# Exp and Gelu ahead of the scaled copy of the head before, and a tenth ring place in place of kept query weights

## The chip, the cores and the metric

The kernel runs on one core of one Trainium2 chip. The metric is the device time of one execution in microseconds; the time before is the median of three runs. Engines are called by the names of the profile: PE (TensorE), DVE (VectorE), ACT (ScalarE), POOL (GpSimd), SP (SyncE). A suffix q is the engine's instruction queue, which also issues DMAs.

## What is computed

One layer of a decoder trunk, on 1024 prompt tokens and 8 x 8 sample tokens, width 1024, all in 32-bit floats. The reference, cut down:

```python
z = x @ w_in                      # q, k, v (8 heads x 64), GLU value and gate (512 each)
att  = dilated window attention   # branches (128,1), (512,4), (2048,16), merged by their denominators
conv = silu(layer_norm(depthwise_conv31(a * sigmoid(g)) + conv_b))
x1 = layer_norm(ALPHA * x + concat(att, conv) @ w_out)

# PEER(x1): product-key choice of experts, 8 heads x 16 experts for each token
q = (x1 @ w_query).reshape(T, 8, 2, 128)
s = einsum('thpc,hpkc->thpk', q, sub_keys)        # 128 keys a side
top_s, top_i = top_k(s, 16)                       # a side
best_s, best_j = top_k(all 16 x 16 sums, 16)      # 16 of 16384 experts
gate = softmax(best_s)
act  = gelu(x1 . expert_u[e])                     # one dot for each token and expert
out  = sum(gate * act * expert_v[e])
y = layer_norm(ALPHA * x1 + out)
```

Further outputs are the new key, value and convolution caches; most of those bytes are copied from DRAM to DRAM.

## The kernel before

**Tiles and places.** The tokens are cut into 9 tiles: 8 prompt tiles of 128 tokens (t = 0 to 7) and one sample tile of 64. All five instruction streams walk the same plan: for n from -1 to 9, for g in 32 groups, for i in 4 places. In round n the experts of tile n are worked off, one slot (one of the 128 experts of each token) at a place, while the front of tile m = n + 1 runs beside them: attention in groups 1 to 9 (one head a group), convolution, output projection and LayerNorm in groups 10 to 15, query projection and the choice of experts from group 15 on. Each stream issues its work of a place in a written order and waits on semaphores, so an instruction that waits holds everything behind it on its engine.

**Experts.** `gather(t, s)` on POOL (L618) fetches 128 rows of 8 KB (u and v of one expert for each token, 1 MB) into a ring of RING = 9 places. On DVE `dot(t, s)` (L1053) makes the dot with x1; after every second slot `gelu` on ACT (L770) applies Gelu to the two results. One place later `weigh` on DVE (L1061, L1064) multiplies by the gates and writes diagonal matrices, and `values_pair` on PE (L1396, L1399, L1403) adds the weighted v rows into PSUM and counts `pv`. A gather waits for the `pv` of the slot that held its ring place. So gelu stands at places i = 1 and 3, weigh and values_pair at i = 2 and 0. Tile 0 has a ring of 4 and `first_values` (L1071 to L1079) on DVE in place of weigh and values_pair.

**Attention of head h in group g.** PE `scores` (L1270, banks 2 and 3, end of group h) -> DVE `weights_max` (L952, L955, i = 2 of group h + 1) -> ACT `weights_exp` (L685, i = 2) -> PE `weights_T` (L1281, i = 3) -> ACT `weights_T` (L694, copy to pT) -> PE `values` (L1292, i = 1 of group h + 2, into bank 2) -> ACT `normalise` (L702, copy scaled by the reciprocal of the sum, i = 1). `values` writes bank 2, which holds the next head's scores until their maximum is taken, and so waits for `sm_done` of head h + 1. `scores` of head h + 2 waits for the scaled copy of head h. In ACT's stream of a group the order is: Gelu (i = 1), scaled copy of head g - 2, Exp of head g - 1 (i = 2), Gelu (i = 3), copy of the transposes of head g - 1 (i = 3). In PE's: values_pair (i = 0), values of head g - 2 (i = 1), values_pair (i = 2), weights_T of head g - 1 and scores of head g (i = 3). ACT also has `ln2_std` (L779), whose result DVE's `ln2_end` (L1106) waits for in group 2.

**Query weights.** Eight blocks of 1 MB, one a head. Block 0 is loaded once from SP's queue (L485) and kept in wq0 for all tiles. The others go through two buffers wq[h % 2], issued from ACT's queue: heads 1 and 2 by `route_loads` (L721) in group 12 (group 18 for the sample tile), head h + 2 after the copy of query h (L751, L753). `queries(m, h)` (L1360) reads them in groups 15, 17, 18, 20, 22, 24, 25 and 27 of a prompt tile.

Of the kernel before, what the change touches and what calls it, by code (L numbers as in the profile page):

```python
# [14 lines left out]
P = 128  # L15
D = 1024
KD = D // P
SEQ = 1024
NB, NT = 8, 8
NS = NB * NT  # L20
# [4 lines left out]
AW = H * E  # L25
# [11 lines left out]
PH = 8  # L37
# [3 lines left out]
KEYC = 128  # L41
# [8 lines left out]
KBLK = NKEY // P  # L50
KEYS = NKEY + NT

RING, FIRST_RING = 9, 4
Z_RING = 4
PAIRS = SLOTS // 2
ROW = 2 * D
# [123 lines left out]
def rows(n):  # L180
    return P if n < PT else NS
# [27 lines left out]
def build(nc, I, O):  # L209
# [5 lines left out]
    with ctx:  # L215
# [3 lines left out]
        def at(off, shape, dt=F32):  # L219
            names[0] += 1  # L220
            return nc.alloc_sbuf_tensor_at(f"t{names[0]}", shape, dt, offset=base + off)

        def sem(name):
            return ctx.enter_context(nc.semaphore(name))
# [22 lines left out]
        wq = at(o_s, [P, 2, KD, 2 * KEYC])  # L247
# [32 lines left out]
        o_l = o_x + 2 * D * 4  # L280
        swapped = at(o_s + 10240, [P, D])

        wq0 = at(o_l, [P, KD, 2 * KEYC])
        lnw2 = at(o_l + 2 * D * 4, [P, 2, D])
        o_k = o_l + 4 * D * 4
        skT = at(o_k, [P, PH * 2, NK])
        o_m = o_k + PH * 2 * NK * 4
        taken = [o_m]
# [37 lines left out]
        sig = at(o_st, [P, 2, 512])  # L326
        q_st = [at(o_st + (2 + i) * 512 * 4, [P, 512]) for i in range(2)]
        assert o_st + 4 * 512 * 4 <= o_x
        glu_st = at(o_l + 2 * D * 4, [P, 3, 512])
        vs = at(o_l + 2 * D * 4 + 3 * 512 * 4, [NS, AW])  # L330

        const_in = sem("const_in")
        bias_in = sem("bias_in")
# [4 lines left out]
        wout_in = sem("wout_in")  # L338
        sk_in = sem("sk_in")
        ln_in = sem("ln_in")  # L340
        wq0_in = sem("wq0_in")
        ln2_in = sem("ln2_in")
        proj_done = sem("proj_done")
        proj_evac = sem("proj_evac")
# [15 lines left out]
        wq_in = [sem(f"wq_in{i}") for i in range(2)]  # L360
# [106 lines left out]
        def _(sp):  # L467
# [14 lines left out]
            sp.dma_start(w_out[:, :, :], I["w_out_t"]).then_inc(wout_in, 16)  # L482
            sp.dma_start(skT[:, :, :], I["skT"]).then_inc(sk_in, 16)
            sp.dma_start(ln1T[:, :, :], I["ln1_t"]).then_inc(ln_in, 16)
            sp.dma_start(wq0[:, :, :], I["wq_t"][0]).then_inc(wq0_in, 16)  # L485

            def copy_cache(i):
                new, old = ((kc_o, I["cache_k_win"]), (vc_o, I["cache_v_win"]))[i % 2]
# [74 lines left out]
            for n in range(TILES + 1):  # L563
                m = n + 1
# [61 lines left out]
        def _(act):  # L626
            def evacuate(u):
                p, _, kind, i, tile = UNITS[u]
                t0, tn, sn = PASSES[p]
                w = tn + sn  # L630
# [50 lines left out]
            def weights_exp(m, h):  # L681
                u = PH * m + h
                L = (m + 1) * P
                act.wait_ge(nm_done, u + 1)
                act.activation(sm[:, u % 2, 0:L], sm[:, u % 2, 0:L], ACT.Exp, bias=soft[:, 2 + u % 2:3 + u % 2], scale=SCALE,  # L685
                               accum_out=soft[:, 4 + u % 2:5 + u % 2]).then_inc(exp_done, 1)

            def weights_T(m, h):
                u = PH * m + h
                L = (m + 1) * P  # L690
                act.wait_ge(p_tr, u + 1)
                if u:
                    act.wait_ge(pv_done, u)
                act.activation(pT[:, 0:L], psum[:, 4 * 512:4 * 512 + L], ACT.Copy).then_inc(pT_ready, 1)  # L694

            def normalise(m, h):
                u = PH * m + h
                act.wait_ge(rd_done, u + 1)
                act.wait_ge(pv_done, u + 1)
                if h == 0 and m:  # L700
                    act.wait_ge(att_tr, m)
                act.activation(att[:, h * E:(h + 1) * E], bank[2][:, 0:E], ACT.Copy, scale=soft[:, 12 + u % 2:13 + u % 2]).then_inc(att_done, 1)  # L702

            def attended(m):
                act.wait_ge(att_tr, m + 1)
                act.activation(mixedT[:, 0:CT, :], bank[4].rearrange("p (c q) -> p c q", c=CT), ACT.Copy).then_inc(att_T, 1)  # L706

            def conv_std(m):
                act.wait_ge(c_var, m + 1)
                act.activation(cstat[0:rows(m), 9:10], cstat[0:rows(m), 8:9], ACT.Sqrt).then_inc(c_std, 1)  # L710


            def route_loads(m):
                if m < PT:
                    act.wait_ge(s_done, PH * (m + 1))
                    act.wait_ge(p_tr, PH * (m + 1))
                else:
                    act.wait_ge(satt_T, 2 * NB)
                act.wait_ge(c_tr2, m + 1)
                for h in (1, 2):  # L720
                    act.dma_start(wq[:, h % 2, :, :], I["wq_t"][h]).then_inc(wq_in[h % 2], 16)  # L721

            def conv_swish(m):
                act.wait_ge(c_tr2, m + 1)
                for c in range(CT):
                    act.activation(mixedT[:, CT + c, 0:rows(m)], bank[2][:, c * P:c * P + rows(m)], ACT.Silu,
                                   bias=cwT[:, c, CK + 2:CK + 3], scale=cwT[:, c, CK + 1:CK + 2]).then_inc(c_T, 1)

            def ln1_std(m):
                act.wait_ge(l_var, m + 1)  # L730
                act.activation(stat[0:rows(m), 17:18], stat[0:rows(m), 16:17], ACT.Sqrt).then_inc(l_std, 1)
# [11 lines left out]
            def x1_rows(m):  # L743
                for half in range(2):
                    act.wait_ge(x1_back, 2 * m + half + 1)
                    act.activation(x1[m % 2][0:rows(m), half * 512:(half + 1) * 512], bank[4 + half][0:rows(m), :], ACT.Copy).then_inc(x1_done, 1)

            def query_copy(m, h):
                r = rows(m)
                act.wait_ge(a_q, PH * m + h + 1)  # L750
                act.activation(qh[:, h % 2, 0:2 * r], bank[2 + h % 2][:, 0:2 * r], ACT.Copy).then_inc(a_qc, 1)  # L751
                if 1 <= h < PH - 2:
                    act.dma_start(wq[:, h % 2, :, :], I["wq_t"][h + 2]).then_inc(wq_in[h % 2], 16)  # L753

            def score_copy(m, h):
# [72 lines left out]
                                x1_rows(PT)  # L828

            def front(m, g, i):  # L830
                if i == 1 and 2 <= g < PH + 2:
                    normalise(m, g - 2)
                if i == 2 and 1 <= g <= PH:
                    weights_exp(m, g - 1)
                if i == 3 and 1 <= g <= PH:
                    weights_T(m, g - 1)
                for h in range(PH):
                    if g == QUERY_AT[h] and i == 3:
                        query_copy(m, h)
                        if h == 0:  # L840
                            x1_rows(m)
                if i != 2:
                    return
                if g == 11:
                    conv_std(m)
                if g == 12:
                    conv_swish(m)
                    attended(m)
                    route_loads(m)
                if g == 14:  # L850
                    ln1_std(m)
                if g == 15:
                    x1_transposed(m)
                for h in range(PH):
                    if g == QUERY_AT[h] + 1:
                        score_copy(m, h)

            for n in range(-1, TILES + 1):
                m = n + 1
# [373 lines left out]
        def _(pe):  # L1233
# [114 lines left out]
            def queries(m, h):  # L1348
                r = rows(m)
                if h == 0:  # L1350
                    pe.wait_ge(x1T_ready, KD * (m + 1))

                if h == 0 and m == 0:
                    pe.wait_ge(wq0_in, 16)
                if h:
                    pe.wait_ge(wq_in[h % 2], 16 * ((4 * m + h // 2 + 1) if h % 2 else (3 * m + h // 2)))
                w_ = wq[:, h % 2, :, :] if h else wq0
                for side in range(2):
                    for k in range(KD):
                        last = pe.matmul(bank[2 + h % 2][:, side * r:(side + 1) * r], w_[:, k, side * KEYC:(side + 1) * KEYC],  # L1360
                                         x1T[:, k, 0:r], start=(k == 0), stop=(k == KD - 1))
                last.then_inc(a_q, 1)
# [119 lines left out]
                                x1_rows(PT)  # L1482

            def front(m, g, i):
                if i == 1 and 2 <= g < PH + 2:
                    values(m, g - 2)
                if i == 3 and 1 <= g < PH + 1:
                    weights_T(m, g - 1)
                if i == 3 and g < PH:
                    scores(m, g)  # L1490
                for h in range(PH):
                    if g == QUERY_AT[h] and i == 3:
                        queries(m, h)
                        if h == 0:
                            x1_rows(m)
                    if g == QUERY_AT[h] + 1 and i == 1:
                        key_scores(m, h)
                if g == 13 and i in (1, 3):
                    out_projection(m, i // 2)
                if i != 1:  # L1500
                    return
                if g == 10:
                    att_transposes(m)
                    conv_rows(m)
                if g == 12:
                    conv_back(m)
                if g == 15:
                    x1_transposes(m)

            for n in range(-1, TILES + 1):  # L1510
                m = n + 1
# [65 lines left out]
```

## Time and profile before

| | |
|---|---|
| median of 3 runs | 3743.29 us (3739.91 to 3750.01) |
| profiled execution | 3747.08 us, its span 3745.3 us |
| busy | DVE 75%, PE 69%, POOL 33%, ACT 18% |
| bytes moved | 1385.68 MB, of them 1140.92 MB by the gathers |
| round n = 0 (tile 0's experts) | from the first gather at 191 us to about 875 us |
| rounds n = 1 to 6 | about 875 to 3080 us |
| round n = 7 (tile 7's experts, sample attention) | about 3080 to 3480 us |
| sample tile's experts | to the end |

In the page and in the tables by stretches, PEclk is the granted TensorE clock as a share of full speed, DMA the mean busy share of the 16 DMA engines, GB/s what they moved. A wait's row reads: who waited, for whom, us in total, times, the longest. In a row of the timeline the number in brackets is the idle time of the engine just before, with what ended it.

### The profile page before, as it was taken

How to read it: one execution, taken by the hardware profiler on the slowest of the kernel's cores; microseconds unless marked ns; L12 is line 12 of the kernel's file. 1: busy time of each engine (PE TensorE's matmuls, PEld its weight loads, DVE VectorE, ACT ScalarE, POOL GpSimd, SP SyncE). 2: the span in 40 equal slices, each digit the busy share in tenths (PEclk: the TensorE clock that was granted, in tenths of full speed). 3: DMA queues.
4: the chain of work that ended last, by engine and by line, in shares of the span. 5: the costliest groups of instructions: out<-in, count | busy, mean ns of one | idle time of the engine just before them, and what ended most of it. 6: DMA issues, size and time to landing. Idle time of an engine off the chain costs nothing.

```text
span 3745.3 us, 39494 instructions
## 1 busy us (share of the span) xinstructions
PE 2592.0 (69%) x13744; PEld 1193.5 (32%) x13744; DVE 2799.2 (75%) x7472; ACT 681.2 (18%) x1478; POOL 1236.1 (33%) x1092
## 2 busy tenths in 40 slices
PE   7864347736775777677677766776787666779766
PEld 5433124532232223233323332333233322234311
DVE  5177867898789868986897689768976894356965
ACT  1210122002200321032013200320132002121000
POOL 0022212123443444434443434344434432233242
PEclk8987668867887888888788888887888878889889
DMA  9977898979999999999999999999989999999698
GB/s 341 343 296 258 303 371 311 400 278 355 398 417 381 361 381 421 395 367 375 415 391 347 381 421 390 344 369 421 393 336 368 420 409 422 418 420 396 261 384 342
DMA packets 217512, 1385.68 MB, mean 370 GB/s; under 512 B 27417, under 2 KB 38169, under 8 KB 66649
## 3 DMA queue, kind: packets, MB, share of 16 engines
q0 software_dynamic: 156672, 1140.92, 76.1%
q1 hardware_dynamic: 40384, 142.88, 10.4%
q10 hardware_dynamic: 20256, 99.35, 6.7%
q8 instruction: 109, 1.79, 0.2%
q14 instruction: 91, 0.74, 0.1%
HBM read 1369.94 MB, written 80.04 MB: 387 GB/s over the span
## 4 chain that ended last, share of the span: by engine, by line
DVE 30%; PE 26%; DMA 25%; issue 13%; ACT 3%; POOL 2%; ACTq 0%; SPq 0%; DVEq 0%; POOLq 0%
DMA t<-in_expert_uv,t 25%; PE psum L1403 12%; DVE t L1053 8%; PE psum L1250 3%; PE psum L1292 3%; DVE psum L1079 2%; PE psum L1328 2%; POOL t L618 2%; PE psum L1360 2%; DVE t L1064 2%; DVE t L1001 2%; DVE t L999 2%; PE psum L1270 2%; DVE t L1002 2%; DVE t L1000 1%
## 5 line engine op out<-in xcount | busy, mean ns | idle before, releaser
L618 POOL DMA_INDIRECT t<-in_expert_uv,t x1088 | 1235.9, 1136 | 2479.9 <-PE psum L1399 982.0
L1403 PE MATMUL psum<-t,t 64*64 64x512 f32 x4576 | 1323.4, 717 | 652.0 <-DVE t L1064 651.4
L1053 DVE CUSTOM_DVE_ANT_0 t<-t,t 128x1024 f32<-128x1024 f32 x1088 | 1322.2, 1222 | 529.6 <-DMA t<-in_expert_uv,t 520.0
L1399 PE MATMUL psum<-t,t 64*64 64x512 f32 x2592 | 807.9, 753 | 0.0
L1403 PEld LDWEIGHTS psum<-t,t 64*64 64x64 f32 x4576 | 329.0, 154 | 1422.6 <-DVE t L1064 798.4
L770 ACT ACTIVATE t<-t 128x2 f32<-128x2 f32 x544 | 110.6, 203 | 2038.0 <-DVE t L1053 2037.0
L1360 PEld LDWEIGHTS psum<-t,t 128*128 128x128 f32 x2304 | 286.3, 206 | 72.2 <-issue 63.4
L1360 PE MATMUL psum<-t,t 128*128 128x128 f32 (+1 forms) x2304 | 296.6, 291 | 4.8 <-ACT t L740 4.8
L1250 PE MATMUL psum<-t,t 128*128 128x128 f32 (+2 forms) x768 | 269.7, 512 | 6.6 <-DMA t<-in_xT 6.1
L920 DVE SCALAR_TENSOR_TENSOR t<-t,t,t 128x128 f32<-128x128 f32 x840 | 238.0, 346 | 0.0
L1292 PE MATMUL psum<-t,t 128*128 128x64 f32 x576 | 105.9, 348 | 162.7 <-issue 162.2
L1399 PEld LDWEIGHTS psum<-t,t 64*64 64x64 f32 x2592 | 182.3, 157 | 0.0
L1250 PEld LDWEIGHTS psum<-t,t 128*128 128x128 f32 x768 | 137.7, 210 | 123.3 <-issue 116.6
L1061 DVE TENSOR_TENSOR t<-t,t 128x2 f32<-128x2 f32 x480 | 75.9, 158 | 128.4 <-ACT t L770 126.3
L1079 DVE SCALAR_TENSOR_TENSOR psum<-t,t,psum 128x1024 f32<-128x1024 f32 x127 | 163.8, 1290 | 4.9 <-DVE t L1071 0.5
L1292 PEld LDWEIGHTS psum<-t,t 128*128 128x128 f32 x576 | 97.3, 256 | 211.1 <-issue 209.9
L1064 DVE TENSOR_TENSOR t<-t,t 128x128 f32<-128x128 f32 x480 | 140.2, 292 | 16.6
L1396 PE MATMUL psum<-t,t 128*64 128x512 f32 x256 | 118.9, 611 | 44.7 <-DVE t L1064 44.7
L1328 PE MATMUL psum<-t,t 128*128 128x512 f32 (+1 forms) x288 | 131.9, 614 | 3.6 <-ACT t L706 3.6
L770 ACT ACT_TABLE_LOAD x103 | 132.1, 1283 | 1.8
L1374 PE MATMUL psum<-t,t 128*128 128x128 f32 (+1 forms) x288 | 53.9, 316 | 112.4 <-ACT t L751 111.9
L1270 PE MATMUL psum<-t,t 64*128 64x512 f32 (+3 forms) x192 | 88.3, 571 | 39.7 <-DMA t<-q_scratch 39.2
(136 smaller groups left out, 2122.2 us busy)
## 6 DMA issues: line engine op xcount, KB each, us to landing
t<-in_wq_t ACTq DMA_DIRECT2D x63, 1024.0 KB, 9.6
out<-in_cache_k_win SPq DMA_DIRECT2D x8, 4080.0 KB, 46.2
out<-in_cache_v_win SPq DMA_DIRECT2D x8, 4080.0 KB, 40.9
t<-in_w_in_t ACTq DMA_DIRECT2D x44, 512.0 KB, 7.5
t<-in_kc_t SPq DMA_DIRECT2D x8, 2560.0 KB, 18.6
t<-in_vc_t SPq DMA_DIRECT2D x8, 2560.0 KB, 14.0
t<-in_expert_uv,t POOLq DMA_INDIRECT x1088, 11.0
t<-in_w_v_t ACTq DMA_DIRECT2D x6, 1024.0 KB, 10.0
```

The lines of the kernel that those rows point to most:

```text
L618: pool.indirect_dma_start(ring[:, r, :], None, I["expert_uv"], bass.IndirectOffsetOnAxis(ap=idn[t % 2][:, s:s + 1], axis=0)).then_inc(land ...
L770: act.activation(d_, d_, ACT.Gelu).then_inc(a_gelu, 1)
L920: dve.scalar_tensor_tensor(dst, src, w, dst, ALU.mult, ALU.add).then_inc(cv, 1)
L1053: dve.tensor_tensor_reduce(out=ring[:, r, 0:D], in0=x1[t % 2][:, :], in1=ring[:, r, 0:D], scale=1.0, scalar=0.0, op0=ALU.mult, op1=ALU.add ...
L1064: dve.tensor_tensor(zt[:, k % Z_RING, :, :], ident2[:, :].unsqueeze(1).broadcast_to([P, 2, NS]), d2.unsqueeze(2).broadcast_to([P, 2, NS]), ...
L1079: dve.scalar_tensor_tensor(first_sum, ring[:, r, D:ROW], w_, first_sum, ALU.mult, ALU.add).then_inc(v_done, 1)
L1250: last = pe.matmul(dst[:, 0:tn + sn], w_ring[:, r, k, :], xT[p][:, k, 0:tn + sn], start=(k == 0), stop=(k == KD - 1))
L1292: last = pe.matmul(bank[2][:, 0:E], pT[:, j * P:(j + 1) * P], v[:, j, h * E:(h + 1) * E], start=(j == 0), stop=(j == m))
L1328: last = pe.matmul(bank[3 - half][0:rows(m), :], mixedT[:, k, 0:rows(m)], w_out[:, k, half * 512:(half + 1) * 512], start=(k == 0), stop=( ...
L1360: last = pe.matmul(bank[2 + h % 2][:, side * r:(side + 1) * r], w_[:, k, side * KEYC:(side + 1) * KEYC], x1T[:, k, 0:r], start=(k == 0), s ...
L1399: last = pe.matmul(AUX[t][half][NS - NS * a:P - NS * a, :], zt[NS * a:NS * a + NS, k % Z_RING, j, :], vv[NS * a:NS * a + NS, :], start=(c ...
L1403: last = pe.matmul(MAIN[t][half][NS * a:NS * a + NS, :], zt[NS * a:NS * a + NS, k % Z_RING, j, :], vv[NS * a:NS * a + NS, :], start=(c == ...
```

## The change

Four edits. On ACT the scaled copy of head g - 2 moves from i = 1 to i = 3 of its group, behind the Exp of head g - 1 and the second Gelu and ahead of the copy of the transposes. On PE values of head g - 2 move from i = 1 to i = 3, behind the second values_pair and ahead of the transposes of head g - 1. Block 0 of the query weights is no longer kept: route_loads loads heads 0 and 1, and head 2 is loaded after the copy of query 0, like the ones after it. The 8 KB a partition that this frees becomes a tenth place of the ring; x1 and what lies behind it move up by as much, lnw2, glu_st and vs keep their addresses.

```diff
--- before.py
+++ after.py
@@ -50,7 +50,7 @@
 KBLK = NKEY // P
 KEYS = NKEY + NT
 
-RING, FIRST_RING = 9, 4
+RING, FIRST_RING = 10, 4
 Z_RING = 4
 PAIRS = SLOTS // 2
 ROW = 2 * D
@@ -280,9 +280,8 @@
         o_l = o_x + 2 * D * 4
         swapped = at(o_s + 10240, [P, D])
 
-        wq0 = at(o_l, [P, KD, 2 * KEYC])
-        lnw2 = at(o_l + 2 * D * 4, [P, 2, D])
-        o_k = o_l + 4 * D * 4
+        lnw2 = at(o_l, [P, 2, D])
+        o_k = o_l + 2 * D * 4
         skT = at(o_k, [P, PH * 2, NK])
         o_m = o_k + PH * 2 * NK * 4
         taken = [o_m]
@@ -326,8 +325,8 @@
         sig = at(o_st, [P, 2, 512])
         q_st = [at(o_st + (2 + i) * 512 * 4, [P, 512]) for i in range(2)]
         assert o_st + 4 * 512 * 4 <= o_x
-        glu_st = at(o_l + 2 * D * 4, [P, 3, 512])
-        vs = at(o_l + 2 * D * 4 + 3 * 512 * 4, [NS, AW])
+        glu_st = at(o_l, [P, 3, 512])
+        vs = at(o_l + 3 * 512 * 4, [NS, AW])
 
         const_in = sem("const_in")
         bias_in = sem("bias_in")
@@ -338,7 +337,6 @@
         wout_in = sem("wout_in")
         sk_in = sem("sk_in")
         ln_in = sem("ln_in")
-        wq0_in = sem("wq0_in")
         ln2_in = sem("ln2_in")
         proj_done = sem("proj_done")
         proj_evac = sem("proj_evac")
@@ -482,7 +480,6 @@
             sp.dma_start(w_out[:, :, :], I["w_out_t"]).then_inc(wout_in, 16)
             sp.dma_start(skT[:, :, :], I["skT"]).then_inc(sk_in, 16)
             sp.dma_start(ln1T[:, :, :], I["ln1_t"]).then_inc(ln_in, 16)
-            sp.dma_start(wq0[:, :, :], I["wq_t"][0]).then_inc(wq0_in, 16)
 
             def copy_cache(i):
                 new, old = ((kc_o, I["cache_k_win"]), (vc_o, I["cache_v_win"]))[i % 2]
@@ -717,7 +714,7 @@
                 else:
                     act.wait_ge(satt_T, 2 * NB)
                 act.wait_ge(c_tr2, m + 1)
-                for h in (1, 2):
+                for h in (0, 1):
                     act.dma_start(wq[:, h % 2, :, :], I["wq_t"][h]).then_inc(wq_in[h % 2], 16)
 
             def conv_swish(m):
@@ -749,7 +746,7 @@
                 r = rows(m)
                 act.wait_ge(a_q, PH * m + h + 1)
                 act.activation(qh[:, h % 2, 0:2 * r], bank[2 + h % 2][:, 0:2 * r], ACT.Copy).then_inc(a_qc, 1)
-                if 1 <= h < PH - 2:
+                if h < PH - 2:
                     act.dma_start(wq[:, h % 2, :, :], I["wq_t"][h + 2]).then_inc(wq_in[h % 2], 16)
 
             def score_copy(m, h):
@@ -828,10 +825,10 @@
                                 x1_rows(PT)
 
             def front(m, g, i):
-                if i == 1 and 2 <= g < PH + 2:
-                    normalise(m, g - 2)
                 if i == 2 and 1 <= g <= PH:
                     weights_exp(m, g - 1)
+                if i == 3 and 2 <= g < PH + 2:
+                    normalise(m, g - 2)
                 if i == 3 and 1 <= g <= PH:
                     weights_T(m, g - 1)
                 for h in range(PH):
@@ -1350,11 +1347,8 @@
                 if h == 0:
                     pe.wait_ge(x1T_ready, KD * (m + 1))
 
-                if h == 0 and m == 0:
-                    pe.wait_ge(wq0_in, 16)
-                if h:
-                    pe.wait_ge(wq_in[h % 2], 16 * ((4 * m + h // 2 + 1) if h % 2 else (3 * m + h // 2)))
-                w_ = wq[:, h % 2, :, :] if h else wq0
+                pe.wait_ge(wq_in[h % 2], 16 * (4 * m + h // 2 + 1))
+                w_ = wq[:, h % 2, :, :]
                 for side in range(2):
                     for k in range(KD):
                         last = pe.matmul(bank[2 + h % 2][:, side * r:(side + 1) * r], w_[:, k, side * KEYC:(side + 1) * KEYC],
@@ -1482,7 +1476,7 @@
                                 x1_rows(PT)
 
             def front(m, g, i):
-                if i == 1 and 2 <= g < PH + 2:
+                if i == 3 and 2 <= g < PH + 2:
                     values(m, g - 2)
                 if i == 3 and 1 <= g < PH + 1:
                     weights_T(m, g - 1)
```

## Rows read from the trace of the kernel before

**Rows 1.** The page: span, and busy time and share of each engine.
```profile
span 3745.3 us, 39494 instructions
PE 2592.0 (69%) x13744; PEld 1193.5 (32%) x13744; DVE 2799.2 (75%) x7472; ACT 681.2 (18%) x1478; POOL 1236.1 (33%) x1092
```

**Rows 2.** By stretches: length, busy PE, PEld, DVE, ACT, POOL; PEclk, DMA, GB/s.
```profile
875.00:3080.00 2205.00, 1581.93 (x9110) 681.00 (x9112) 1813.16 (x5095) 440.08 (x937) 881.04 (x758) 0.83 0.96 386
1245.00:1608.00 363.00, 261.81 (x1490) 108.80 (x1490) 301.07 (x843) 71.82 (x159) 151.99 (x129) 0.83 0.97 395
3080.00:3480.00 400.00, 312.60 (x2172) 125.95 (x2169) 208.18 (x501) 79.38 (x158) 121.01 (x110) 0.89 0.99 411
```

**Rows 3.** The same for attention of tiles 2 and 5 and two later stretches.
```profile
885.00:959.00 74.00, 51.16 (x262) 18.88 (x258) 64.34 (x201) 28.07 (x50) 31.08 (x26) 0.82 0.92 358
1988.00:2074.00 86.00, 64.17 (x331) 30.57 (x328) 62.94 (x180) 32.02 (x50) 28.10 (x26) 0.81 0.86 318
2112.00:2160.00 48.00, 39.85 (x228) 16.88 (x228) 27.67 (x59) 12.45 (x30) 20.15 (x19) 0.95 1.01 421
2200.00:2300.00 100.00, 64.78 (x456) 32.55 (x452) 94.44 (x275) 7.17 (x28) 40.13 (x36) 0.80 1.00 410
```

**Rows 4.** Waits between 875 and 3080 us.
```profile
POOL t L618 <- PE psum L1399: 982.0, 303, 8.6
...
DVE t L1053 <- DMA t<-in_expert_uv,t: 176.0, 153, 4.7
...
DVE t L1061 <- ACT t L770: 117.0, 40, 5.8
DVE t L1106 <- ACT t L779: 22.9, 6, 5.6
```

**Rows 5.** Timeline of tile 6's attention: start, us, engine, line, operation.
```profile
2391.89 1.08 DVE L952 CUSTOM_DVE_ANT_0 t<-psum,t 128x896 f32<-128x896 f32 x1
...
2393.08 3.22 PE L1292 MATMUL psum<-t,t 128*128 128x64 f32 x14 [3.38 <-issue]
...
2395.28 1.22 DVE L1053 CUSTOM_DVE_ANT_0 t<-t,t 128x1024 f32<-128x1024 f32 x1
...
2396.23 1.12 PE L1403 MATMUL psum<-t,t 64*64 64x512 f32 x2
...
2396.40 0.31 ACT L702 ACTIVATE t<-psum,t 128x64 f32<-128x64 f32 x1 [6.85 <-PE psum L1292]
...
2396.73 1.28 ACT L685 ACT_TABLE_LOAD   x1
...
2398.03 1.04 ACT L685 ACTIVATE t<-t,t 128x896 f32<-128x896 f32 x1
...
2399.18 1.28 ACT L770 ACT_TABLE_LOAD   x1
...
2400.23 0.94 POOL L618 DMA_INDIRECT t<-in_expert_uv,t  x1 [7.66 <-PE psum L1399]
2400.47 0.20 ACT L770 ACTIVATE t<-t 128x2 f32<-128x2 f32 x1
2400.71 0.16 DVE L1061 TENSOR_TENSOR t<-t,t 128x2 f32<-128x2 f32 x1 [4.20 <-ACT t L770]
...
2400.76 1.77 PE L1270 MATMUL psum<-t,t 64*128 64x512 f32 x4
```

**Rows 6.** DMA queues and issues: packets, MB, share; count, KB each, us to landing.
```profile
q0 software_dynamic: 156672, 1140.92, 76.1%
...
t<-in_wq_t ACTq DMA_DIRECT2D x63, 1024.0 KB, 9.6
```

**Rows 7.** Timeline of ACT in tile 5: the copies of queries 0 and 2.
```profile
2154.28 0.39 ACT L751 ACTIVATE t<-psum 128x256 f32<-128x256 f32 x1 [5.13 <-PE psum L1360]
...
2184.60 0.38 ACT L751 ACTIVATE t<-psum 128x256 f32<-128x256 f32 x1 [1.30 <-PE psum L1360]
```

**Rows 8.** The chain between 56 and 105 us, shares by line.
```profile
by line: PE psum L1250 40.1%; issue 12.7%; DVE t L944 9.8%; PE psum L1270 9.1%; PE psum L1292 7.7%; ACT t L685 7.6%; PE psum L1281 7.2%; ACT L685 2.6%; ACT t L702 1.8%; DVE t L952 1.3%; ACT t L651 0.7%; DVE t L955 0.3%; ACTq L699 0.2%
```

## What I predicted, and how

> **What bounds the kernel now.** I read the page first, then a table by stretches, then the waits inside the long stretch, and last one attention head in order of time. On the page no compute engine is full: VectorE (DVE) is busy 75% of the span and TensorE 69% [rows 1]. The table by stretches shows why that average says little. Six prompt tiles run from 875 to 3080 us, 2205 us in all, with the DMA engines busy 0.96 of the time at 386 GB/s [rows 2]. That looks like a DMA limit, but inside a tile it is one only in part. In the stretch behind attention (2112 to 2160) the engines move 421 GB/s, which I take as their rate when they never run dry; DVE is there busy only 27.67 of 48 us. In the second half of a tile, where the experts are chosen (2200 to 2300), DVE is full (94.44 of 100 us) and the DMA engines are nearly so (410 GB/s). During attention (885 to 959, 1988 to 2074) neither is: DVE is busy 64.34 of 74 and 62.94 of 86 us, and only 358 and 318 GB/s move [rows 3]. So attention is where time can be had.
>
> The waits name the cause. In the six tiles DVE waits 117.0 us for the Gelu (L770) and 22.9 us for the square root of the second LayerNorm (L779), both on ScalarE (ACT); it waits 176.0 us for rows still on their way. GpSimd waits for a ring place to come free for longer than DVE waits for rows [rows 4]: in these phases the transfers are held back by the engines, not the engines by transfers.
>
> One head (tile 6, head 3) shows the chain [rows 5]. DVE ends the masked maximum at 2393.0. TensorE's queue has stood before values() for 3.38 us, because that instruction needs this very maximum (scores and values share PSUM bank 2). The 14 matmuls take 3.22 us, the scaled copy (L702) follows at 2396.40 and takes 0.31, and only then does ACT begin on the Exp: table 1.28, Exp 1.04, table for Gelu 1.28, Gelu 0.20. DVE has ended its last dot at 2396.50 and gets the Gelu at 2400.71: 4.20 us idle. Beside that, values_pair() for the ring stands behind values() and starts at 2396.23, and GpSimd issues its next gather at 2400.23 after 7.66 us. But neither Exp nor Gelu reads anything of head h-1's values or scaled copy; they only stand behind them in ACT's order.
>
> **The change, part by part.** (a) ACT: Exp(h) and Gelu go ahead of the scaled copy of head h-1. From 2393.0 the Exp can start at once. Removed ahead of the Gelu is the row of values plus the copy plus their hand-offs: from 2393.08 to the table load at 2396.73, 3.65 us for 14 matmuls [rows 5]. That is 0.23 us a matmul and 0.4 fixed; tile m has 2(m+1) matmuls, so the piece is 1.8, 2.3, 2.7, 3.2, 3.65 and 4.1 us in tiles 2 to 7, 17.75 in sum. Six Gelu waits in each tile, 36 in all, carry nearly the whole 117.0 us [rows 4]. Without a floor at zero the pieces would take off 6 x 17.75 = 106; in each tile about two of six waits are shorter than the piece, so I take 94 and leave 23. In the head shown 4.20 becomes about 0.6. The LayerNorm root also stands behind an Exp, once a tile: of 22.9 us I take 17 away. Gross: 111 us of DVE idle.
>
> What comes late next: Gelu still arrives about 4 us after the maximum (two tables, Exp, Gelu: 2396.73 to 2400.67 in the rows), and DVE has a dot, a block of taps and a dot, about 3.5 us, to fill it. So the cover is nearly as long as the wait.
>
> (b) TensorE: values(h-1) moves behind the values_pair() of place i = 2, directly before the transposes of head h. That pair no longer stands behind values(), so its ring places come free some 3 to 5 us earlier; values() still needs the maximum, but now what is queued behind it is the transposes, which need the Exp 2.6 us later. scores() of the next head, the last thing queued there, needs the scaled copy, which now comes after the Gelu, some 4.5 us after the maximum. Its matmuls take 1.77 us [rows 5], so scores stand ready about 6.5 us after one maximum, and the next maximum comes 11 us after it (1988 to 2074 are six heads, 14.3 us each [rows 3], less 3.2). Cost nothing, with 4 us of cover.
>
> (c) Weights of head 0 come anew in every tile. The page had 63 such 1 MB loads on ACT's queue and one kept on SP's [rows 6]; now it is 72 and none, eight more. One is 1.05 MB, 2.5 us of all engines at the 421 GB/s of [rows 3]. The load falls where route_loads stands, at the head of the 421 GB/s stretch, so little hides it: 8 x 2.5 = 20 us as the upper bound, and zero as the lower if it falls beside idle transfers, as it may in tile 1 and the sample tile. I take 20. Head 2's weights are now asked for after the copy of query 0 (2154.28) and needed some 4 us ahead of the copy of query 2 (2184.60) [rows 7], about 26 us later, against a landing of 9.6 [rows 6]: nothing waits. The first tile loses its early load and gets block 0 beside block 1, from the same spot in route_loads, three groups ahead of its use: I cost that at nothing too. The issue itself is one more instruction in a queue that is mostly idle (ACT is busy 18% [rows 1]).
>
> (d) A tenth ring place. Gathers of even slots wait for the same pair as before; those of odd slots for one pair less. While DVE keeps pace nothing is won. Where DVE-bound work hands over to the 421 GB/s stretch, one more gather is already there: 1140.92 MB over 1088 gathers [rows 6] is 1.05 MB, at most 2.5 us a tile, 17 us over seven handovers. At least it is zero. I take 10, the middle, since both ends are equally near.
>
> (e) Start. In the first tile's attention (56 to 105 us) values and scaled copy lie in the chain itself: 7.7% and 1.8% of 49 us [rows 8], so up to 4.7 us go; I take 4. The attention of tile 1, which runs beside tile 0's gathers, I take at nothing, between -5 (same saving) and +8, since the scaled copy now stands behind a Gelu whose dots wait for rows there.
>
> Of the 111 us in (a) not all is time. With six waits shortened, 24 slots take 86 - 18 = 68 us instead of 86, a demand of 318 x 86/68 = 402 GB/s with everything else that moves: close to 421. The tiles' 851 MB (386 x 2205) plus 6.3 MB of new weights would need 2086 us even at the 411 GB/s that the sample's stretch holds for 400 us [rows 2], so the six tiles can shrink by at most 119. The lightest one, 363 us at 395 GB/s, has only 14 us to that rate. I take 80% of the 111, 90 us.
>
> The Trainium skill speaks against this part: "DMA: Bandwidth & Descriptors", section Bandwidth, puts the HBM side at about 358 GB/s for one core when both cores of a pair stream. By it attention, already at 318 to 358, would have little to give. The 421 GB/s in [rows 3] disagree here, where one core runs. A second rule: "ScalarE: Activation LUTs", What ACT_TABLE_LOAD costs, gives 1283 ns and a drain of some 1380 more for each switch. The trace agrees on the first (1.28) and shows no room for the second [rows 5]; by the page two switches would leave each Gelu wait about 2.8 us longer.
>
> Sum: -90 + 20 - 10 - 4 = -84. The profiled span 3745.3 becomes 3661. The execution took 3747.1 in all, 1.8 more than its span, and 3.8 more than the median of 3743.3; so the median should come to 3659, and I say 3660.
>
> **The rivals.** First, rows instead of Gelu, the slower side: the DMA engines are the real bound and attention's idle transfers cannot be used, because near 400 GB/s a gather lands later. Then each microsecond of Gelu wait comes back as a wait of L1053 on its row, and the 8 MB count in full: 3743 + 20 - 3 = 3760. It decides if the rate in attention stays near 350. For it speaks the 0.96 share [rows 2]; against it the 421 GB/s and the 7.66 us for which GpSimd had nothing to issue.
>
> Second, half is swallowed: either the demand of 402 GB/s is met only in part, or the scaled copy behind the Gelu pushes scores() late, so that the maximum (L952) waits. The gain is then 45 in place of 90: 3743 - 45 + 20 - 10 - 4 = 3704. The 4 us of cover speak against the latter, the lightest tile's small room speaks for the former.
>
> Third, more than forecast: all 111 us become time and the ring gives its 17: 3743 - 111 + 20 - 17 - 4 = 3631. TensorE could help, as its 3 to 4 us gaps close and its granted clock of 0.81 [rows 3] rises.
>
> Fourth, the reordering doesn't do what it says: L1061's wait stays where it is since another wait holds the Exp. The weights and ring then decide alone: 3743 + 20 - 10 = 3753, or within 0.3% with a better ring.
>
> **How the numbers follow.** Forecast (3640 to 3690) 0.62; half swallowed 0.17; more than forecast 0.09; rows instead of Gelu 0.07; no effect 0.05. The range 3628 to 3708 takes in the third and the second and leaves about 2 in 10 outside. A measurement of this kernel tells about 0.3%, 11 us, from no change: faster needs a time under 3732. Faster 0.87, same 0.06, slower 0.07.
>
> **What would show it.** In the changed profile: L1061's wait for L770 falls from 117.0 to about 25 in the six tiles, L1106's from 22.9 to about 6; L702 follows L770; a head takes about 11 us in place of 14; GB/s in attention rises to between 370 and 400; L721 and L753 have 72 loads; DVE's wait for rows rises from 176.0 by no more than about 40. The six tiles shrink by 80 us or so. I am wrong if L1053's wait grows as much as L1061's falls, or if L952 begins to wait for L1270.

## The result: more gain than the range held

The changed kernel takes 3618.6 us (median of 4, 3613.5 to 3624.0) against 3746.7 us of the kernel before on the same chip: ratio 0.966, 95% interval 0.9635 to 0.9686. The range was 3628 to 3708, the forecast 3660. The direction was as forecast and so was the wait that went away; the size was not: 84 us of span forecast, 123 us measured (3745.3 to 3622.1).

The page after the change (line numbers are three lower than before, and six lower from TensorE's query projection on, which takes in values_pair): DVE is 77% busy where it was 75% [rows 1].

```profile
span 3622.1 us, 39510 instructions
PE 2522.6 (70%) x13744; PEld 1154.6 (32%) x13744; DVE 2795.8 (77%) x7472; ACT 678.4 (19%) x1478; POOL 1267.3 (35%) x1092
...
t<-in_wq_t ACTq DMA_DIRECT2D x72, 1024.0 KB
```

By stretches, with the columns of [rows 2]: the six prompt tiles, attention of tile 2, attention of tile 5, the stretch behind it, and the choice of experts.

```profile
869.28:2960.00 2090.72, 1514.84 (x9114) 645.79 (x9116) 1811.64 (x5100) 440.02 (x941) 909.25 (x758) 0.86 1.00 411
880.00:944.00 64.00, 46.77 (x278) 16.50 (x274) 63.28 (x199) 27.11 (x50) 30.30 (x26) 0.89 1.01 420
1938.60:2001.90 63.30, 52.84 (x334) 25.53 (x330) 61.90 (x177) 31.36 (x50) 29.99 (x25) 0.92 0.99 399
2001.90:2060.00 58.10, 42.63 (x233) 16.44 (x230) 38.91 (x92) 13.10 (x27) 27.07 (x22) 0.88 1.01 422
2150.00:2250.00 100.00, 67.53 (x432) 29.06 (x432) 94.97 (x282) 6.40 (x26) 38.08 (x36) 0.81 1.01 416
```

The stretch that was 875 to 3080 in [rows 2] is now 869 to 2960. It is 114 us shorter; some 6 of the 123 us lie ahead of it and 3 behind. Attention of tile 5 takes 63.3 us where the same six heads took 86 [rows 3], and the DMA engines move 399 GB/s there, not 318. DVE does the same work (61.90 us against 62.94) and is now busy for 98% of the stretch. So attention has become DVE's in full, and the DMA engines are at 1.00 over the six tiles, at the 411 GB/s from which the prediction worked out that they could shrink by 119 us at most.

The waits in that stretch, to be read against [rows 4] and this row of the kernel before:

```profile
DVE t L917 <- DMA t<-glu_scratch: 1.6, 3, 0.6
```
```profile
POOL t L615 <- PE psum L1393: 860.2, 281, 9.8
DVE t L1050 <- DMA t<-in_expert_uv,t: 189.5, 151, 3.8
...
DVE t L914 <- DMA t<-glu_scratch: 9.2, 4, 2.7
DVE t L1058 <- ACT t L767: 2.8, 8, 0.6
DVE t L1103 <- ACT t L776: 2.1, 5, 0.6
```

The wait for Gelu fell from 117.0 to 2.8 us, not to 23, and that for the LayerNorm root from 22.9 to 2.1: 135.0 us of DVE idle in place of the 111 forecast. Waits for rows rose by 13.5 us, and those for the convolution's input (L914, L917 before) from 1.6 to 9.2. 135.0 - 13.5 - 7.6 = 113.9, against 114 us by which the stretch shrank (2205 to 2091): the waits of DVE account for the whole.

Why nothing was left of the Gelu wait is in one head of tile 6, in order of time:

```profile
2310.09 0.20 ACT L767 ACTIVATE t<-t 128x2 f32<-128x2 f32 x1 [2.05 <-DVE t L1050]
2310.31 1.28 ACT L682 ACT_TABLE_LOAD   x1
...
2312.63 1.08 DVE L949 CUSTOM_DVE_ANT_0 t<-psum,t 128x896 f32<-128x896 f32 x1
...
2313.75 0.15 DVE L952 TENSOR_SCALAR t<-t 128x1 f32<-128x1 f32 x1
...
2313.94 1.04 ACT L682 ACTIVATE t<-t,t 128x896 f32<-128x896 f32 x1 [2.35 <-DVE t L952]
...
2315.09 1.28 ACT L767 ACT_TABLE_LOAD   x1
...
2316.39 0.20 ACT L767 ACTIVATE t<-t 128x2 f32<-128x2 f32 x1
2316.50 0.30 ACT L699 ACTIVATE t<-psum,t 128x64 f32<-128x64 f32 x1
...
2317.16 0.15 DVE L1058 TENSOR_TENSOR t<-t,t 128x2 f32<-128x2 f32 x1
```

The load of the Exp table runs at 2310.31, straight behind the Gelu of place 1 and 2.3 us before the maximum even starts. Then ACT waits 2.35 us for the maximum, and the Exp follows it by 0.04 us. Before the change the scaled copy, which waits, stood ahead of that load, and the load came behind the wait (2396.73 in [rows 5]). Gelu now ends 0.57 us before DVE wants it. Over the 48 heads of tiles 2 to 7 it ends on average 2.7 us after the maximum (L952), where it was 6.0 us before.

### The profile page after: what moved, and what is told of

Read it like the earlier page. It is cut to its first block, busy times and chain, and to the rows that moved or that the text cites. A ratio compares the mean times of both kernels' runs of the same rounds, so it can differ in the third digit from the quotient of the medians.

```text
span 3622.1 us, 39510 instructions
## 1 busy us (share of the span) xinstructions
PE 2522.6 (70%) x13744; PEld 1154.6 (32%) x13744; DVE 2795.8 (77%) x7472; ACT 678.4 (19%) x1478; POOL 1267.3 (35%) x1092
## 4 chain that ended last, share of the span: by engine, by line
DVE 40%; DMA 30%; PE 17%; issue 11%; ACT 1%; POOL 1%; SPq 0%; ACTq 0%; DVEq 0%; POOLq 0%
DMA t<-in_expert_uv,t 28%; DVE t L1050 12%; PE psum L1397 7%; DVE t L917 4%; PE psum L1247 3%; DVE psum L1076 3%; PE psum L1325 3%; DVE t L1061 2%; DVE t L998 2%; DVE t L996 2%; DVE t L999 2%; DVE t L997 2%; DMA t<-glu_scratch 1%; DVE t L995 1%; PE psum L1390 1%
## 5 line engine op out<-in xcount | busy, mean ns | idle before, releaser
L615 POOL DMA_INDIRECT t<-in_expert_uv,t x1088 | 1267.1, 1165 | 2320.9 <-PE psum L1393 860.2
L1397 PE MATMUL psum<-t,t 64*64 64x512 f32 x4576 | 1288.7, 702 | 697.4 <-DVE t L1061 692.8
L1397 PEld LDWEIGHTS psum<-t,t 64*64 64x64 f32 x4576 | 324.6, 151 | 1485.7 <-DVE t L1061 868.5
L1393 PE MATMUL psum<-t,t 64*64 64x512 f32 x2592 | 782.6, 733 | 0.0
L1354 PEld LDWEIGHTS psum<-t,t 128*128 128x128 f32 x2304 | 279.6, 202 | 70.5 <-issue 62.5
L1354 PE MATMUL psum<-t,t 128*128 128x128 f32 (+1 forms) x2304 | 290.0, 287 | 4.8 <-ACT t L737 4.8
L917 DVE SCALAR_TENSOR_TENSOR t<-t,t,t 128x128 f32<-128x128 f32 x840 | 238.0, 345 | 0.0
L1393 PEld LDWEIGHTS psum<-t,t 64*64 64x64 f32 x2592 | 178.7, 153 | 0.0
L1247 PEld LDWEIGHTS psum<-t,t 128*128 128x128 f32 x768 | 136.0, 208 | 122.7 <-issue 114.9
L1368 PE MATMUL psum<-t,t 128*128 128x128 f32 (+1 forms) x288 | 53.2, 313 | 120.2 <-ACT t L748 119.9
L1289 PE MATMUL psum<-t,t 128*128 128x64 f32 x576 | 84.6, 296 | 59.5 <-issue 58.9
L1289 PEld LDWEIGHTS psum<-t,t 128*128 128x128 f32 x576 | 76.4, 207 | 112.0 <-issue 110.8
L1245 PE MATMUL psum<-t,t 128*128 128x256 f32 (+1 forms) x288 | 82.0, 451 | 32.1 <-ACT t L632 20.7
```

What stands on the lines that cost most here:

```text
L615: pool.indirect_dma_start(ring[:, r, :], None, I["expert_uv"], bass.IndirectOffsetOnAxis(ap=idn[t % 2][:, s:s + 1], axis=0)).then_inc(land ...
L917: dve.scalar_tensor_tensor(dst, src, w, dst, ALU.mult, ALU.add).then_inc(cv, 1)
L1247: last = pe.matmul(dst[:, 0:tn + sn], w_ring[:, r, k, :], xT[p][:, k, 0:tn + sn], start=(k == 0), stop=(k == KD - 1))
L1289: last = pe.matmul(bank[2][:, 0:E], pT[:, j * P:(j + 1) * P], v[:, j, h * E:(h + 1) * E], start=(j == 0), stop=(j == m))
L1393: last = pe.matmul(AUX[t][half][NS - NS * a:P - NS * a, :], zt[NS * a:NS * a + NS, k % Z_RING, j, :], vv[NS * a:NS * a + NS, :], start=(c ...
L1397: last = pe.matmul(MAIN[t][half][NS * a:NS * a + NS, :], zt[NS * a:NS * a + NS, k % Z_RING, j, :], vv[NS * a:NS * a + NS, :], start=(c == ...
```

## The experiments

All ratios are to the kernel before in runs on the same chip in the same session. The kernel before took 3745.6, 3744.3 and 3746.0 us in the three sessions, so that times of different sessions can be compared to a few us. Lines of code are shown as edits to the kernel named.

### The order alone

The kernel before with the two moves of the change; ring of nine, kept weights.

```diff
 # ACT, front()
-                if i == 1 and 2 <= g < PH + 2:
-                    normalise(m, g - 2)
                 if i == 2 and 1 <= g <= PH:
                     weights_exp(m, g - 1)
+                if i == 3 and 2 <= g < PH + 2:
+                    normalise(m, g - 2)
 # PE, front()
-                if i == 1 and 2 <= g < PH + 2:
+                if i == 3 and 2 <= g < PH + 2:
                     values(m, g - 2)
```

> The kernel before with the new order on ACT and PE alone; ring of nine and kept head-0 weights stay. Theory A (the order is the whole gain; eight more 1 MB loads cost about 2.5 us each, 20 us, and the tenth ring place gives back at most 2.5 us at each of about seven handovers, 17 us): between 3600 and 3620, at or a little under the changed kernel, L1061-type Gelu waits near 3 us in the six tiles. Theory B (the tenth place is what lets the DMA engines reach 421 GB/s in attention, so that a large part of the gain is the ring's): 3650 or more, with the DMA share in attention under 0.95.

Measured: 3625.5 us, ratio 0.9697 (0.9672 to 0.9721), 120 us under the kernel before. It is 5 us above the range of theory A and far under B; DVE's Gelu waits are 3.0 us over five whole tiles (the stretch of the tables further down), as A says, where the kernel before has 91.3. The changed kernel, run again beside it, took 3621.3.

### The changed kernel again

> The changed kernel once more on the same chip as the three beside it, so that differences of some 10 us can be read: 3619 within 5 by every theory.

Measured: 3621.3 us, ratio 0.9674 (0.9653 to 0.9695). The intervals of this and of the order alone overlap: whether the memory part of the change brings anything on top of the order can't be told.

### Ring and weights alone

The changed kernel with the old order, the reverse of the edit above.

> The changed kernel with the old order on ACT and PE: tenth ring place and head-0 weights loaded in every tile alone. Theory A: 3746 + 20 - 10 = 3756, between 3748 and 3766 (no faster than before), Gelu waits stay near 117 us. Theory B: 3710 or less, since ring places are what attention lacks.

Measured: 3735.4 us, ratio 0.9978 (0.9963 to 0.9993). Neither range held it. Gelu waits stayed, as theory A says: 88.7 us over the five tiles. But with the old order the memory part is worth 10 us, not minus 10: the ring gives more than the loads cost.

### A ring of nine in the changed kernel

```diff
-RING, FIRST_RING = 10, 4
+RING, FIRST_RING = 9, 4
```

> The changed kernel with a ring of nine; the loads of head 0's weights stay. It prices the tenth place. Theory A: 5 to 20 us above the changed kernel, 3624 to 3639, the same amount appearing as DVE's wait for rows. Theory B: 40 us or more above it.

Measured: 3648.5 us, ratio 0.9749 (0.9729 to 0.9769), 27 us above the changed kernel (3621.3): between the two ranges. This one run prices both halves of the memory part, in the new order. Against the order alone, which differs in the weights only, it is 23.0 us longer for eight loads: 2.9 us each, where the four times of the order alone lie 15 us apart. Against the changed kernel the tenth place is worth 27 us. The three steps, -120 + 23 - 27, lead from the kernel before to the changed one and must add up to its -124; the sum is no test of them.

### A ring of eight

```diff
-RING, FIRST_RING = 10, 4
+RING, FIRST_RING = 8, 4
...
-        o_x = o_ring + RING * ROW * 4
+        o_x = o_ring + 10 * ROW * 4
```

> The changed kernel with gathers going through eight of the ten ring places; all addresses behind the ring stay. Nine places cost 27 us against ten. If a place is worth one gather at each handover from DVE's pace to the DMA engines' pace, eight cost another 20 to 30, 3668 to 3679. If the loop of issue, landing, dot and release begins to limit the rate in attention, the loss grows: 3690 or more, with the DMA share of the six tiles under 0.97.

Measured: 3699.9 us, ratio 0.9896 (0.9869 to 0.9923): 51 us above nine places. Five whole tiles, from the store of tile 0's rows to that of tile 5's, in the order changed kernel, nine places, eight places:

```profile
885.91:2649.40 1763.49, 1275.71 (x7635) 540.02 (x7634) 1527.16 (x4308) 367.60 (x790) 773.27 (x641) 0.87 1.00 410
```
```profile
889.32:2669.47 1780.15, 1280.14 (x7621) 539.64 (x7622) 1531.75 (x4308) 367.58 (x788) 773.78 (x640) 0.86 0.99 406
```
```profile
883.66:2694.59 1810.93, 1291.03 (x7609) 545.07 (x7609) 1534.75 (x4308) 367.61 (x788) 751.06 (x639) 0.85 0.98 399
```

DVE's waits for rows in the same three stretches:

```profile
DVE t L1050 <- DMA t<-in_expert_uv,t: 160.0, 129, 3.8
```
```profile
DVE t L1050 <- DMA t<-in_expert_uv,t: 176.7, 151, 3.7
```
```profile
DVE t L1050 <- DMA t<-in_expert_uv,t: 206.2, 184, 4.5
```

DVE's work is the same within 8 us; the rate falls from 410 to 406 to 399 GB/s and the time grows by 16.7 and 30.8 us. The waits for rows grow by 16.7 and 29.5 us, nearly all of it. A place is not worth a fixed gather at each handover: the loss grows with each place taken, and it stands in more than one part of a tile. With ten places 90 us of tile 3's attention and convolution (1243 to 1333 us) move 418 GB/s and 100 us of its choice of experts (1443 to 1543) 413; with nine the same stretches, 9 us later, move 407 and 404. In the 60 us behind the first both move 421. That speaks for a loop of issue, landing, dot and release that runs short of places.

The DMA share of the five tiles is 0.98, where I had asked for less than 0.97 of that theory. An earlier form of the run, which gave no time, had asked for 0.93 or less in attention; it is 0.97 in tile 5 here. So the sign that I had named did not come. The share does fall with the rate, though: 410 / 1.00, 406 / 0.99 and 399 / 0.98 are 410, 410 and 407, about the same bytes for each busy microsecond. Whether each place costs more than the one before is less sure than that each costs through the tiles: places come free two at a time, so from ten to nine one half of the gathers waits for another pair, and from nine to eight the other half. That was not taken apart.

### ACT's order alone, and TensorE's alone

Both are the changed kernel with the other engine's move taken back.

> The changed kernel with TensorE's order as before (values at place 1, ahead of the second values_pair); ACT's new order, ring and weights stay. Theory A (ACT's order carries the gain, since only Exp and Gelu stood in DVE's chain): Gelu waits near 3 us as in the changed kernel, and 3620 to 3640. Theory C (the ring places that come free 3 to 5 us earlier in attention carry a good part): 3660 or more, with the DMA share in attention back under 0.95.

Measured: 3630.1 us, ratio 0.9699 (0.9672 to 0.9727), as theory A says. Gelu waits are 2.7 us over the five tiles. ACT's order carries nearly all; TensorE's move adds 9 to 12 us at most, and the intervals overlap. The five tiles between two stores took 1761.8 us here and 1763.5 in the changed kernel, so in those tiles TensorE's move is worth nothing that shows.

> The changed kernel with ACT's order as before (scaled copy at place 1, ahead of the Exp); TensorE's new order, ring and weights stay. To be read against the kernel with the old order and the same memory (3735). Theory A: the Exp still waits for values through the scaled copy, so Gelu waits stay at 110 us or more and the time is 3725 to 3760. Theory C: 3700 or less, as the second values_pair no longer stands behind values.

Measured: 3789.0 us, ratio 1.012 (1.0097 to 1.0143), outside both ranges: alone, TensorE's move costs 54 us against the same memory with the old order (3735.4). One head of tile 4 of this kernel:

```profile
1725.00 0.81 DVE L949 CUSTOM_DVE_ANT_0 t<-psum,t 128x640 f32<-128x640 f32 x1
...
1726.59 0.59 PE L1397 MATMUL psum<-t,t 64*64 64x512 f32 x2
...
1727.12 1.33 PE L1289 MATMUL psum<-t,t 128*128 128x64 f32 x10
...
1728.55 0.31 ACT L699 ACTIVATE t<-psum,t 128x64 f32<-128x64 f32 x1 [6.94 <-PE psum L1289]
1728.88 1.28 ACT L682 ACT_TABLE_LOAD   x1
...
1732.64 0.16 DVE L1058 TENSOR_TENSOR t<-t,t 128x2 f32<-128x2 f32 x1 [4.35 <-ACT t L767]
```

The maximum ends at 1725.82, but values begin only at 1727.12, behind the values_pair that now stands ahead of them. With ACT's old order the scaled copy, the table load, the Exp and the Gelu hang on those values. A part of the 1.3 us comes back: the ten matmuls of values take 1.33 us here behind the pair, and 2.37 in the kernel with the old order and the same memory, where TensorE has been idle for 4.41 us ahead of them, so that DVE waits 4.35 us in this head and 4.18 in that kernel. Over the 42 values of tiles 2 to 7 that follow a maximum they begin on average 1.65 us after it instead of at once and take 1.45 us instead of 1.93, and the Gelu comes 1.2 us later. The five whole tiles are 50.9 us longer than in that kernel (1891.04 and 1840.11). DVE's waits for Gelu and root grow by 33.2 and 8.1 of these; another 15.0 are waits for the convolution's input, of which I haven't followed the cause. Once the scaled copy is behind the Gelu, nobody in that chain waits for values, and the same move costs nothing that shows.

### The table load put back into the chain, and its control

One more instruction of 128x1 ahead of each Exp from tile 2 on. It waits for the same maximum. As a Gelu it keeps the Gelu table active, and the Exp's load comes behind it; as an Exp it leaves the load where it is, ahead of the wait.

```diff
                 act.wait_ge(nm_done, u + 1)
+                if m >= 2:
+                    act.activation(soft[:, 14:15], ident[:, 0:1], ACT.Gelu)   # control: ACT.Exp
```

> The changed kernel with one extra Gelu of 128x1 on ACT ahead of each Exp from tile 2 on, which waits for the same maximum; so the Exp's table load (1.28 us) comes after the wait and not before it. Nothing else changes; the output is the same. Theory T (my prediction left the table load in the chain, while in the new order it runs ahead of the wait; that is the missing part of the gain): 1.5 us come back to the chain, cover of 0.6 us in tile 6 is used up, Gelu waits of 25 to 45 us in the six tiles and 10 to 35 us more time, 3630 to 3655. Rival (the table load is hidden anyway; the excess gain is DVE's or TensorE's): within 5 us of the changed kernel, Gelu waits under 10.

Measured: 3651.1 us, ratio 0.9754 (0.9734 to 0.9775). A head of tile 6:

```profile
2330.92 0.15 DVE L954 TENSOR_SCALAR t<-t 128x1 f32<-128x1 f32 x1
2331.11 0.20 ACT L683 ACTIVATE t<-t 128x1 f32<-128x1 f32 x1 [3.65 <-DVE t L954]
2331.32 1.28 ACT L684 ACT_TABLE_LOAD   x1
2332.61 1.04 ACT L684 ACTIVATE t<-t,t 128x896 f32<-128x896 f32 x1
...
2333.77 1.28 ACT L769 ACT_TABLE_LOAD   x1
2335.06 0.20 ACT L769 ACTIVATE t<-t 128x2 f32<-128x2 f32 x1
2335.30 0.16 DVE L1060 TENSOR_TENSOR t<-t,t 128x2 f32<-128x2 f32 x1 [0.89 <-ACT t L769]
```

and the wait over 868 to 2990 us:

```profile
DVE t L1060 <- ACT t L769: 40.9, 42, 2.0
...
DVE t L1105 <- ACT t L778: 10.4, 6, 2.1
```

The load is behind the maximum again, DVE waits 0.89 us in this head, and Gelu waits are 40.9 us in place of 2.8. Time and waits lie in the ranges of theory T.

> Control for the run with the small Gelu ahead of each Exp: the same extra instruction of 128x1, with the same wait, but an Exp, so that the table load stays ahead of the wait and only the instruction itself (0.2 us) enters the chain. Theory T (the 30 us there were the table load's 1.28 us a head): within 8 us of the changed kernel, 3615 to 3629, Gelu waits under 12 us in the six tiles. Rival (any extra instruction behind the maximum costs as much): 3640 or more.

Measured: 3616.9 us, ratio 0.9667 (0.9646 to 0.9688), no different from the changed kernel (3618.6 and 3621.3). The extra instruction costs nothing that shows; the place of the 1.28 us load costs 34 us (3651.1 - 3616.9). Over the five tiles the profiles say the same: waits for Gelu and root are 32.3 + 9.6 us with the small Gelu and 4.6 + 2.5 with the small Exp, 34.8 apart. The profile with the small Gelu also has one wait of 15.1 us for the convolution's input. That one isn't the load's: the changed kernel's second profile has one of 15.2. In all, these waits are 1.6 to 3.3 us in the profiles with nine places (before, order alone, ring of nine) and 5.8 to 22.6 in those with ten; why is open.

## Why the prediction was too small

**What bounds attention: right.** DVE's waits for Gelu and for the root were the time to be had, they stood behind values and the scaled copy, and they went. The rival "rows instead of Gelu" fell: attention moved 399 GB/s and the waits for rows rose by 13.5 us. The rival "doesn't do what it says" fell with the Gelu waits. The Trainium skill's figure of some 358 GB/s ("DMA: Bandwidth & Descriptors", section Bandwidth) is given there for both cores of a pair streaming. One core runs here, so it did not speak against this part as I had it, and it is no limit: six tiles ran at 411 GB/s.

**The step that failed first: "What comes late next: Gelu still arrives about 4 us after the maximum (two tables, Exp, Gelu ...)".** It kept the Exp table's load in the chain; on average the Gelu ends 2.7 us after the maximum. The 4.20 us of the example should have become nothing and not 0.6; over the six tiles 135.0 us of idle went, 24 more than the 111 of the sum. The run with the load put back and its control show that this term is real: 34 us. They show more: with the load in the chain, as I had it, 40.9 + 10.4 = 51.3 us of these waits are left, where I left 29. The small Gelu of 0.20 us is in that, but not all of the 22. So my 111 was too much for the chain that I had in mind, and the load that I had wrongly in it more than made up for that. The kernel with the load in the chain takes 3651.1 us, 9 from the forecast; that is in part luck, since the ring in it gives 17 more than I took. I had written that Exp "can start at once", and then added a load that has no operand to wait for. A second figure of the Trainium skill, the drain of 1380 ns after each load ("ScalarE: Activation LUTs", What ACT_TABLE_LOAD costs), doesn't show here either: the Exp runs from 2313.94 to 2314.98, the load starts at 2315.09 and Gelu at 2316.39, 1.30 us later.

**"Not all is time", 80%: a little low.** The order alone gives 120 us, where I had 94 (90 in the six tiles and 4 at the start). Of the 26 missing, most is the first step: 80% of 135 is 108, 18 more than my 90. In the changed kernel 21 of 135 us came back as waits, 16%, and that includes the new loads.

**Eight loads of 1 MB: right.** 20 us forecast, 23.0 measured, with nine places and the new order.

**The tenth ring place: wrong in kind.** I counted one gather of 2.5 us at each of seven handovers, 17 us at most, and took 10 as the middle (that would be 8.5). It is 27 us in the new order, and the ninth is worth 51. Places count in attention and in the choice of experts, not only at a handover, so the ring's length is part of the rate. The miss between 84 and 124 us is 26 for the order, 17 for the ring and -3 for the loads.

**TensorE's move: right for this change, by half a reason.** "Cost nothing" held: nothing shows in the five tiles. But I argued it from what stands behind values, and didn't ask who waits for values itself. In the old order of ACT that is the Exp, and there the same move costs 54 us.

**The start: within noise.** The first store of a tile's rows came 8 us earlier in the profiled run (885.9 against 894.0), against 4 forecast, but repeats of the same kernel differ by 6 there (879.4 in the second).

**The bounds.** My upper case (3631) counted every one of the 111 us and 17 for the ring and no error in either figure. I had worked out both myself, from one head and from one model of the ring. The range should have gone below them. Of the rivals "more than forecast" came nearest, for other reasons than its own: the gain was in a step that it shared with the forecast, and in the ring.

## What to carry to other kernels

An instruction that waits holds back what is behind it even if that needs no operand: here it was an activation table's load. When an order is changed, list for every instruction of the chain whether it now stands ahead of the wait or behind it, the ones without operands too. Place such a load so that the engine's next wait comes after it. And before a move is costed at nothing, ask who waits for the moved instruction, under the order of the other engines that is to stand beside it.

## What the runs showed of the hardware

In these kernels a table load is not held back by its ACTIVATE's wait: it ran 3.6 us ahead of the Exp that it serves and took 1.28 us in either place. With ten, nine and eight ring places the busy share of the DMA engines falls from 1.00 to 0.99 and 0.98 and the rate from 410 to 406 and 399 GB/s, so 47 us in 1763 are only two hundredths of share. TensorE's granted clock in the attention of tile 5, a mean between its two levels, rose from 0.81 to 0.92. It is 0.89 with only ACT in the new order, and 0.97 with both in the new order but the old ring and weights. The six heads take 63.3, 63.3 and 63.4 us at 0.92, 0.89 and 0.97, so between these three the clock set nothing there.
